# Unread identity products at four places of a hybrid decoder step: two stage ends after a feed forward and projections, one inside the index scores, one after the selection

## The chip, the cores and the metric

The kernel runs on one core of a Trainium2 chip. The metric is the device time of one execution in microseconds (us); a smaller time is better. Three executions of the kernel before took 3087.32 us in the median (3080.42 to 3089.07). A core has five engines that run side by side and wait for each other through semaphores: TensorE (PE in the profile), VectorE (DVE), ScalarE (ACT), GpSimd (POOL) and SyncE (SP), whose queue here issues most of the transfers.

## The reference

One layer of a decoder serves 1024 prompt tokens and 8 sample sequences of 4 tokens (1056 tokens in all, model width 1024).

```python
x = x + 0.5 * swiglu(rms_norm(x, ffn1_norm), ffn1_w_gate, ffn1_w_up, ffn1_w_down)      # D_FF = 2816
h = rms_norm(x, mix_norm)
q, k, v, qi, ki, wi, hq, hf, hi, hg, ga, gr = split_cols(h @ w_in)
# A: index scores I[t,s] = sum_h w[t,h] * relu(qi[t,h] . ki[s]) choose min(256, L/4) causal keys,
#    attention over the chosen keys (own keys for the prompt; paged cache plus 4 own keys for the samples)
# B: HGRN2 gated linear recurrence with a matrix state
merged = sigmoid(ga) * (att @ w_branch_attn) + sigmoid(gr) * (rec @ w_branch_hgrn)
x = x + merged @ w_out
x = x + 0.5 * swiglu(rms_norm(x, ffn2_norm), ffn2_w_gate, ffn2_w_up, ffn2_w_down)
```

Outputs are x for prompt and samples, the new keys, values, index keys, and the recurrence states.

## The kernel before

The step is a chain of stages; each stage is one `Block` with its own program for each engine, and between two Blocks stands a barrier: in the program every engine first drains what it has issued, then reports, and no engine passes before all five have reported. The profile shows the first instruction of a new Block as released by "PEq L69". The stages are: the first feed forward (tiles named `ff_`), the token projections (`tok_`), the index scores (`idx_`), the selection with further projections (`sel_`), the attention (`att_`), the recurrence (`hg_`), the merge, and the second feed forward.

Products in full precision are split: each weight and each activation is held as a high and a low part, and `split_product` (L97 to L99) issues three products for one. In the first feed forward the hidden width goes by in pairs of 128; tokens go in three chunks of 384, 384 and 288. Its last round (`LAST`) also prepares the next norm: when the down products of a chunk have been added to x (DVE, L580), ACT squares them (L341), POOL adds the squares up over eight slices (L298, `gathered`), PE sums over partitions with a product with ones (`sums`, L725), DVE makes the variance (L526) and the root, scales x (L542), and ACT and DVE write the high and low part of h (L360, L551). The last such series, for chunk 2, is the end of the stage.

The token projections go through nine weight chunks; each needs a load, ACT for the high part (L1043) and POOL for the low part (`tok_wlo`, L1001). PE starts a chunk when POOL has done it. Finished 128x256 results are turned by PE (`turn`, L1014) three steps later; the last transfer stores the turned queries.

The index scores first turn the index pages of the sample sequences on PE (`turn`, L1270) and score them (L1280), then ACT and DVE make the weighted relu of the sample part (`sample_relu`, `sample_part`, L1387, L1390), PE adds it over heads with a product with `sel` (L1308), and then come 48 steps over prompt tiles and heads: PE scores (L1322, L1324), ACT relu (L1366), DVE multiply and add (L1403, L1406).

The selection is a bisection on DVE beside 28 column blocks of projections on PE (L97 to L99, `sel_proj`). The attention begins by turning cached key pages on PE (L1772), and SP issues the loads of further pages one by one (L1679).

`idle_products` (L102 to L105) issues products of the identity with itself, 128 columns in 32-bit floats, whose result nobody reads. The kernel before has them at eight places, among them 12 at the start of the token projections, 36 and 16 in the index scores.

```python
def idle_products(nc, out, ident, count):
    for _ in range(count):
        nc.tensor.matmul(out, ident[:, :], ident[:, :], start=True, stop=True)
```

Of the kernel before, what the change touches and what calls it, by code (L numbers as in the profile page):

```python
# [29 lines left out]
P = 128  # L30
# [71 lines left out]
# [4 lines that stand above are left out]
# [3 lines left out]
QS = 2 * NCH  # L109
# [4 lines left out]
def feed_forward(nc, tag, xT, hhi, hlo, gain, w_gate, w_up, w_down, ident, ones, x_in=None, gain_row=None, next_gain=None,  # L114
# [10 lines left out]
    LAST = PAIRS - 1  # L125
    E0 = NCH if x_in is not None else 0
    with Scope(nc, tag) as s:
# [10 lines left out]
        gu = s.ps("gu", [P, 2, 2, 512])  # L138
# [544 lines left out]
        def _(pe):  # L683
# [123 lines left out]
            if next_gain is None:  # L807
                for q in range(QS):
                    gate_up(LAST, q)
            else:  # L810
                pe.wait_ge(ones_set, 1)
                for q in range(3):
                    gate_up(LAST, q)
                for j in range(KD):
                    down(LAST, j)
                gate_up(LAST, 3)
                gate_up(LAST, 4)
                sums(NCH)
                for j in range(KD, 2 * KD):
                    down(LAST, j)  # L820
                gate_up(LAST, 5)
                sums(NCH + 1)
                for j in range(2 * KD, 3 * KD):
                    down(LAST, j)
                sums(NCH + 2)
            if y_out is not None:
                n = 0
                for j in range(OUTS_PER):
                    down(LAST, j)
                    c = j // KD  # L830
                    if c and j % KD == 1 or j == OUTS_PER - 1:
                        while n < tiles_within(c - 1 if j < OUTS_PER - 1 else c):
                            turn_back(n)
                            n += 1
# [29 lines left out]
def token_projections(nc, hhi, hlo, w_in, q_gain, k_gain, cos, sin, ident, qT_d, kT_d, qiT_d, kiT_d, wi_d, hv_d,  # L864
# [10 lines left out]
    with Scope(nc, "tok") as s:  # L875
# [128 lines left out]
        @block.tensor  # L1004
        def _(pe):
            def turn(m):
                if m < 0 or m >= M or not turns(m):
                    return
                x = count(turns, m)
                if x >= 2:  # L1010
                    pe.wait_ge(kept_done, x - 1)
                pe.wait_ge(out_done, m + 1)
                for b in range(1 if kind(m) == "ki" else 2):
                    last = nc.tensor.transpose(turned[:, x % 2, b, :], out[:, m % 4, b * P:(b + 1) * P], ident[:, :])  # L1014
                last.then_inc(turn_done, 1)

            idle_products(nc, proj[:, 3, 0:P], ident, 12)
            for m in range(M):
                c, n = STEPS[m]
                w = width(c)  # L1020
                if n == 0:
                    pe.wait_ge(w_lo_done, c + 1)
                if m >= 4:
                    pe.wait_ge(take_done, m - 3)
                tok = slice(n * P, (n + 1) * P) if n < TILES else slice(T - P, T)
                for k in range(KD):
                    ps = proj[:, m % 4, 0:w]
                    nc.tensor.matmul(ps, hhi[:, k, tok], whi[:, c % WS, k, 0:w], start=(k == 0), stop=False)
                    nc.tensor.matmul(ps, hhi[:, k, tok], wlo[:, c % WS, k, 0:w], start=False, stop=False)
                    last = nc.tensor.matmul(ps, hlo[:, k, tok], whi[:, c % WS, k, 0:w], start=False, stop=(k == KD - 1))  # L1030
                last.then_inc(proj_done, 1)
                turn(m - 3)
            for m in range(M - 3, M):
                turn(m)

        @block.scalar
        def _(act):
# [140 lines left out]
def index_scores(nc, scores, qiT_d, kiT_d, wi_d, pages, pages_in, same_token, new_floor, ident):  # L1178


    with Scope(nc, "idx") as s:
# [79 lines left out]
        def _(pe):  # L1261
# [38 lines left out]
                                 lambda r: k_hi[r, cols], lambda r: k_lo[r, cols])  # L1300
                last.then_inc(seq_scored, 1)

            idle_products(nc, turned[:, 0, 0:P], ident, 16)
            pe.wait_ge(sel_in, 16)
            pe.wait_ge(sample_part, 2)
            for x in range(3):
# [105 lines left out]
FEATS = 32  # L1412


def select_keys_and_project(nc, scores, masks, hhi, hlo, w_in, feat_d, table, pages, pages_in, cache_k):

# [3 lines left out]
    with Scope(nc, "sel") as s:  # L1422
# [13 lines left out]
        bitf = s.sb("bitf", [P, SLABS])  # L1436
        thr = s.sb("thr", [P, SLABS], I32)
        proj = s.ps("proj", [P, 2, NCH, 512])
        w_loaded = [s.sem(f"w_loaded{n}") for n in range(2)]
        w_hi_done, w_lo_done = s.sem("w_hi_done"), s.sem("w_lo_done")  # L1440
        proj_done, proj_read, kept_done = s.sem("proj_done"), s.sem("proj_read"), s.sem("kept_done")
# [50 lines left out]
        @block.tensor  # L1492
        def _(pe):
            def body(n, i, pair, first):
                for u in range(2):
                    pe.wait_ge(w_lo_done, 2 * pair + u + 1)
                    for c in range(NCH):
                        cols, w_c = slice(CHUNK[c][0], CHUNK[c][0] + CHUNK[c][1]), CHUNK[c][1]
                        if not first:
                            pe.wait_ge(proj_read, 6 * pair + 3 * u + c - 5)  # L1500
                        for k in range(KD):
                            w = slice(k * P, (k + 1) * P)
                            last = split_product(nc, proj[:, u, c, 0:w_c], whi[:, u, w], wlo[:, u, w], hhi[:, k, cols],
                                                 hlo[:, k, cols], k == 0, k == KD - 1)
                        last.then_inc(proj_done, 1)

            sections(pe, body)

        @block.scalar
        def _(act):  # L1510
# [1442 lines left out]
def build(nc, a, o):  # L2953
# [9 lines left out]
    with Scope(nc, "core") as s:  # L2963
# [6 lines left out]
        with Scope(nc, "front") as front:  # L2970
# [7 lines left out]
            with Scope(nc, "proj") as proj:  # L2978
                with Scope(nc, "fetch") as fetch:
                    idx_pages = fetch.sb("idx_pages", [P, DB * PAGES, HD])  # L2980
                    token_projections(nc, hhi, hlo, a["w_in"], a["q_norm"], a["k_norm"], a["t_cos"], a["t_sin"], ident,
                                      scratch["qT"], scratch["kT"], scratch["qiT"], scratch["kiT"], scratch["wi"],
                                      scratch["hv"], rows["k_prompt"], rows["k_sample"], rows["v_prompt"], rows["v_sample"],
                                      rows["idx_k_prompt"], rows["idx_k_sample"], table, a["page_table"], idx_pages,
                                      idx_pages_in, a["cache_idx_k"])
                    scores = proj.sb("scores", [P, SLABS, SW], side="right")
                    index_scores(nc, scores, scratch["qiT"], scratch["kiT"], scratch["wi"], idx_pages, idx_pages_in,
                                 a["t_same_token"], a["t_new_floor"], ident)
                mix = Scope(nc, "mix").__enter__()
                masks = mix.sb("masks", [P, SLABS, SW], mybir.dt.bfloat16)  # L2990
                pages = mix.sb("pages", [P, SLOTS * PAGES, KV * HD])
                select_keys_and_project(nc, scores, masks, hhi, hlo, a["w_in"], scratch["feat"], table, pages, first_pages_in,
                                        cache_k)
        attention(nc, scratch["mixed"], masks, pages, first_pages_in, table, scratch["qT"], scratch["kT"], rows["v_prompt"],
                  rows["v_sample"], cache_k, cache_v, a["t_causal"], a["t_own"], ident, values_in)
        mix.__exit__(None, None, None)
# [82 lines left out]
```

## Time and profile before

| | |
|---|---|
| median of three runs | 3087.32 us (3080.42 to 3089.07) |
| the profiled execution: time, span in the trace | 3090.39 us, 3088.7 us |
| PE, DVE, ACT, POOL busy | 94%, 50%, 23%, 19% |
| mean granted TensorE clock | 0.957 |
| idle products in the trace | 956 records of 478 products |

Times in the trace are microseconds from the start of the span. A row of the order of time gives start, time taken, engine, line, operation, the tile written and the tiles read, the shape, and in brackets how long the engine had been idle and who released it. A full-precision 32-bit product is recorded as two MATMUL records. The granted clock is a share of full speed: 1.00 is 2.4 GHz, 0.50 is 1.2 GHz.

### The profile page before, as it was taken

The page shows a single profiled execution, that of the slowest core. Times are in us where ns is not written, and L with a number is a line of the kernel's source. Part 1 is how long each engine was busy: PE and PEld are TensorE (multiplying, and loading weights), DVE is VectorE, ACT ScalarE, POOL GpSimd, SP SyncE. Part 2 cuts the span into 40 slices and gives each one's busy share as a digit, 9 for nine tenths or more (in the row PEclk, how much of TensorE's full clock was granted, in tenths as well). Part 3 has the DMA queues.
Part 4 walks back from the last instruction along what each step waited for, and adds up shares of the span by engine and source line. Part 5 has one row for each costly group of instructions (what it writes and reads, how often), then busy time and mean ns, then how long its engine had stood idle before and what let it go on. Part 6 is the DMA issues. An engine that isn't in the chain of part 4 may idle for free. (4 is left out here: it accounts for less than half of the span.)

```text
span 3088.7 us, 50931 instructions
## 1 busy us (share of the span) xinstructions
PE 2907.8 (94%) x19321; PEld 2810.8 (91%) x19321; DVE 1530.8 (50%) x3429; ACT 699.6 (23%) x1351; POOL 575.5 (19%) x330
## 2 busy tenths in 40 slices
PE   8999999999699986999989988879989999999998
PEld 7999999999699965999958987778979999999998
DVE  5333322223767639999924657656444222233323
ACT  5111111111323235222113444321032111111110
POOL 0121221112311012122132111122002111122120
PEclk9999999999799998999987998789999999999999
DMA  4111111111223112243263141225211111111111
GB/s 126 42 56 53 41 54 41 41 41 41 78 78 109 47 45 55 90 144 115 86 168 94 25 144 58 75 69 159 76 49 55 41 41 41 41 48 61 41 34 57
DMA packets 239301, 212.93 MB, mean 69 GB/s; under 512 B 26978, under 2 KB 216578, under 8 KB 239042
## 3 DMA queue, kind: packets, MB, share of 16 engines
q1 hardware_dynamic: 230594, 182.35, 19.9%
q10 hardware_dynamic: 4608, 17.30, 1.4%
q0 software_dynamic: 3968, 11.54, 1.4%
q8 instruction: 81, 1.33, 0.2%
q14 instruction: 50, 0.41, 0.0%
HBM read 167.94 MB, written 43.21 MB: 68 GB/s over the span
## 5 line engine op out<-in xcount | busy, mean ns | idle before, releaser
L271 POOL TENSOR_TENSOR ff_wlo<-ff_raw,ff_whi 128x1024 fp32r<-128x1024 f32 x124 | 298.6, 2429 | 1203.6 <-ACT ff_whi L369 1202.5
L567 DVE TENSOR_TENSOR ff_prod<-ff_silu,ff_gu 128x384 f32<-128x384 f32 x132 | 68.8, 521 | 806.8 <-ACT ff_silu L374 806.8
L97 PE MATMUL ff_dn<-ff_ahi,ff_whi 128*128 128x384 f32 (+1 forms) x1056 | 340.4, 322 | 8.2 <-DVE ff_alo L573 3.8
L97 PE MATMUL ff_gu<-front_hhi,ff_whi 128*128 128x384 f32 (+1 forms) x1056 | 340.6, 323 | 2.6 <-DVE front_hlo L511 2.3
L99 PE MATMUL ff_gu<-front_hhi,ff_wlo 128*128 128x384 f32 (+1 forms) x1056 | 339.4, 321 | 0.0
L98 PE MATMUL ff_gu<-front_hlo,ff_whi 128*128 128x384 f32 (+1 forms) x1056 | 339.4, 321 | 0.0
L99 PE MATMUL ff_dn<-ff_ahi,ff_wlo 128*128 128x384 f32 (+1 forms) x1056 | 339.2, 321 | 0.0
L98 PE MATMUL ff_dn<-ff_alo,ff_whi 128*128 128x384 f32 (+1 forms) x1056 | 339.2, 321 | 0.0
L97 PE MATMUL ff_gu<-rear_hhi,ff_whi 128*128 128x384 f32 (+1 forms) x1056 | 338.8, 321 | 0.0
L98 PE MATMUL ff_gu<-rear_hlo,ff_whi 128*128 128x384 f32 (+1 forms) x1056 | 338.6, 321 | 0.0
L99 PE MATMUL ff_gu<-rear_hhi,ff_wlo 128*128 128x384 f32 (+1 forms) x1056 | 338.5, 321 | 0.0
L374 ACT ACTIVATE ff_silu<-ff_gu 128x384 f32<-128x384 f32 x132 | 61.4, 466 | 864.7 <-PE ff_gu L99 864.7
L97 PE MATMUL sel_proj<-front_hhi,sel_whi 128*128 128x384 f32 (+1 forms) x672 | 216.8, 323 | 14.5 <-POOL sel_wlo L1488 14.5
L369 ACT ACTIVATE ff_whi<-ff_raw 128x1024 fp32r<-128x1024 f32 x132 | 132.6, 1053 | 374.3 <-PE ff_dn L99 285.1
L98 PE MATMUL sel_proj<-front_hlo,sel_whi 128*128 128x384 f32 (+1 forms) x672 | 216.6, 322 | 0.0
L99 PE MATMUL sel_proj<-front_hhi,sel_wlo 128*128 128x384 f32 (+1 forms) x672 | 216.5, 322 | 0.0
L97 PEld LDWEIGHTS ff_dn<-ff_ahi,ff_whi 128*128 128x128 f32 x1056 | 198.7, 188 | 10.4 <-DVE ff_alo L573 4.4
L97 PEld LDWEIGHTS ff_gu<-front_hhi,ff_whi 128*128 128x128 f32 x1056 | 198.7, 188 | 3.1 <-DVE ff_wlo L516 3.0
L98 PEld LDWEIGHTS ff_dn<-ff_alo,ff_whi 128*128 128x128 f32 x1056 | 198.7, 188 | 0.1
L98 PEld LDWEIGHTS ff_gu<-front_hlo,ff_whi 128*128 128x128 f32 x1056 | 198.8, 188 | 0.0
L99 PEld LDWEIGHTS ff_dn<-ff_ahi,ff_wlo 128*128 128x128 f32 x1056 | 198.7, 188 | 0.0
L99 PEld LDWEIGHTS ff_gu<-front_hhi,ff_wlo 128*128 128x128 f32 x1056 | 198.7, 188 | 0.0
(336 smaller groups left out, 6236.9 us busy)
## 6 DMA issues: line engine op xcount, KB each, us to landing
ff_raw<-in_ffn_w_gate SPq DMA_DIRECT2D x44, 512.0 KB, 3.7
ff_raw<-in_ffn_w_up SPq DMA_DIRECT2D x44, 512.0 KB, 3.7
ff_raw<-in_ffn_w_down SPq DMA_DIRECT2D x44, 512.0 KB, 3.4
scratch_feat<-sel_stage ACTq DMA_DIRECT2D x32, 528.0 KB, 2.7
sel_raw<-in_w_in SPq DMA_DIRECT2D x28, 512.0 KB, 3.7
merge_gates<-scratch_feat SPq DMA_DIRECT2D x48, 176.0 KB, 2.7
tok_raw<-in_w_in SPq DMA_DIRECT2D x8, 1024.0 KB, 6.5
mix_pages<-in_cache_k SPq DMA_DIRECT2D x64, 128.0 KB, 2.1
```

Of the source, the lines that this page charges most:

```text
L97: nc.tensor.matmul(out, w_hi, x_hi, start=first, stop=False)
L98: nc.tensor.matmul(out, w_hi, x_lo, start=False, stop=False)
L99: return nc.tensor.matmul(out, w_lo, x_hi, start=False, stop=last)
L271: nc.gpsimd.tensor_tensor(wlo[:, u, :], raw[:, u % RAW, :], whi[:, u, :], ALU.subtract).then_inc(w_lo_done, 1)
L369: nc.scalar.activation(whi[:, u, :], raw[:, u % RAW, :], ACT.Copy).then_inc(w_hi_done, 1)
L374: nc.scalar.activation(act_out[:, q % 2, 0:w], gu[:, q % 2, 0, 0:w], ACT.Silu).then_inc(silu_done, 1)
L567: nc.vector.tensor_tensor(prod[:, 0:w], act_out[:, b, 0:w], gu[:, b, 1, 0:w], ALU.mult).then_inc(prod_done, 1)
```

## The change

`idle_products` is called at five more points, and one call grows. In the first feed forward's last round 26 are put before the last eight down products (behind a wait that `prod_done` has reached the fifth product of that round), 28 after them, and 84 after the last `sums`. At the end of the token projections stand 30, behind a wait for `take_done`. In the index scores the 16 before the product with `sel` become 76. At the end of the selection stand 26, into a bank of PSUM that is added for them.

```diff
@@ feed_forward, block.tensor
                 gate_up(LAST, 5)
                 sums(NCH + 1)
+                pe.wait_ge(prod_done, QS * LAST + 5)
+                idle_products(nc, gu[:, 0, 0, 0:P], ident, 26)
                 for j in range(2 * KD, 3 * KD):
                     down(LAST, j)
+                idle_products(nc, gu[:, 0, 0, 0:P], ident, 28)
                 sums(NCH + 2)
+                idle_products(nc, gu[:, 0, 0, 0:P], ident, 84)
@@ token_projections, block.tensor
             for m in range(M - 3, M):
                 turn(m)
+            pe.wait_ge(take_done, M - 3)
+            idle_products(nc, proj[:, M % 4, 0:P], ident, 30)
@@ index_scores, block.tensor
-            idle_products(nc, turned[:, 0, 0:P], ident, 16)
+            idle_products(nc, turned[:, 0, 0:P], ident, 76)
             pe.wait_ge(sel_in, 16)
             pe.wait_ge(sample_part, 2)
@@ select_keys_and_project
         proj = s.ps("proj", [P, 2, NCH, 512])
+        unread = s.ps("unread", [P, 512])
...
             sections(pe, body)
+            idle_products(nc, unread[:, 0:P], ident, 26)
```

`ident` is handed to `select_keys_and_project` as one more argument. No other engine's program changes, and no transfer.

The order of PE's instructions at the end of the first feed forward (`ff_`) and the start of the token projections (`tok_`), before; the two branches are the passage from Block to Block with its barrier:

```order
1346 L99 MATMUL ff_dn<-ff_ahi,ff_wlo 128x288
1347 L725 MATMUL ff_dn<-ff_raw,core_ones 128x288
1348 L69 UNCONDITIONAL_BRANCH
1349 L1004 UNCONDITIONAL_BRANCH
1350 L105 MATMUL tok_proj<-core_ident 128x128 x12
```

The same place now:

```order
1347 L99 MATMUL ff_dn<-ff_ahi,ff_wlo 128x288
1348 L105 MATMUL ff_gu<-core_ident 128x128 x28
1349 L725 MATMUL ff_dn<-ff_raw,core_ones 128x288
1350 L105 MATMUL ff_gu<-core_ident 128x128 x84
1351 L69 UNCONDITIONAL_BRANCH
1352 L1008 UNCONDITIONAL_BRANCH
1353 L105 MATMUL tok_proj<-core_ident 128x128 x12
```

28 products have moved in before the last sums, and 84 between the sums and the barrier.

PE in the index scores (`idx_`), between the last sample sequence and the product with `sel`, before:

```order
3428 L1280 MATMUL idx_big<-idx_k_hi,idx_wide_lo 128x4 x2
3429 L105 MATMUL idx_turned<-core_ident 128x128 x16
3430 L1308 MATMUL idx_big<-idx_relus,idx_sel 128x512 x2
3431 L1308 MATMUL idx_big<-idx_relus,idx_sel 128x4
3432 L1322 MATMUL idx_big<-idx_k_hi,idx_q_both 128x384
```

and now:

```order
3432 L1286 MATMUL idx_big<-idx_k_hi,idx_wide_lo 128x4 x2
3433 L105 MATMUL idx_turned<-core_ident 128x128 x76
3434 L1314 MATMUL idx_big<-idx_relus,idx_sel 128x512 x2
3435 L1314 MATMUL idx_big<-idx_relus,idx_sel 128x4
3436 L1328 MATMUL idx_big<-idx_k_hi,idx_q_both 128x384
```

The order is the same; 60 more products stand ahead of the product with `sel`.

## Rows read from the trace of the kernel before

**Rows 1.** The page: PE's busy time, and its granted clock in 40 slices.

```profile
PE 2907.8 (94%) x19321; PEld 2810.8 (91%) x19321; DVE 1530.8 (50%) x3429; ACT 699.6 (23%) x1351; POOL 575.5 (19%) x330
PEclk9999999999799998999987998789999999999999
```

**Rows 2.** Instructions in order of time, PE, end of the first feed forward.

```profile
790.50 0.81 PE L725 MATMUL ff_dn<-ff_raw,core_ones 128*128 128x384 f32 x2
795.09 0.40 PE L97 MATMUL ff_dn<-ff_ahi,ff_whi 128*128 128x288 f32 x1 [3.78 <-DVE ff_alo L573]
...
805.42 0.30 PE L98 MATMUL ff_dn<-ff_alo,ff_whi 128*128 128x288 f32 x1
805.56 0.29 PE L99 MATMUL ff_dn<-ff_ahi,ff_wlo 128*128 128x288 f32 x1
810.78 1.33 PE L725 MATMUL ff_dn<-ff_raw,core_ones 128*128 128x288 f32 x2 [4.93 <-POOL ff_raw L298]
822.55 4.86 PE L105 MATMUL tok_proj<-core_ident 128*128 128x128 f32 x24 [10.44 <-PEq L69]
...
839.99 0.58 PE L1028 MATMUL tok_proj<-tok_whi,front_hhi 128*128 128x256 f32 x1 [2.28 <-POOL tok_wlo L1001]
```

**Rows 3.** The same view, DVE, same stretch.

```profile
798.75 0.82 DVE L580 SCALAR_TENSOR_TENSOR x_xT<-ff_dn,x_xT 128x288 f32<-128x288 f32 x2
...
812.27 0.44 DVE L526 TENSOR_SCALAR ff_room<-ff_dn 128x288 f32<-128x288 f32 x1
...
819.55 2.67 DVE L551 TENSOR_TENSOR front_hlo<-ff_room,front_hhi 128x1152 fp32r<-128x1152 f32 x2
```

**Rows 4.** PE across the passage from token projections to index scores.

```profile
1089.76 0.41 PE L1014 MATMUL tok_turned<-core_ident,tok_out 128*128 128x128 f32 x2 [0.73 <-DVE tok_out L1152]
1095.02 3.68 PE L1270 MATMUL idx_turned<-core_ident,fetch_idx_pages 128*64 128x128 f32 x32 [4.86 <-PEq L69]
1098.63 8.81 PE L105 MATMUL idx_big<-core_ident 128*128 128x128 f32 x72
1107.37 1.97 PE L1270 MATMUL idx_turned<-core_ident,fetch_idx_pages 128*64 128x128 f32 x32
```

**Rows 5.** PE in the index scores, before and after the product with `sel`.

```profile
1135.12 3.84 PE L105 MATMUL idx_turned<-core_ident 128*128 128x128 f32 x32
1146.34 3.97 PE L1308 MATMUL idx_big<-idx_relus,idx_sel 128*128 128x512 f32 x6 [7.38 <-DVE idx_relus L1390]
1150.56 0.59 PE L1322 MATMUL idx_big<-idx_k_hi,idx_q_both 128*128 128x384 f32 x1 [0.25 <-DVE proj_scores L1394]
```

**Rows 6.** PE, end of the selection and start of the attention.

```profile
1540.68 0.29 PE L99 MATMUL sel_proj<-front_hhi,sel_wlo 128*128 128x288 f32 x1
1545.46 1.94 PE L1772 MATMUL att_turned<-core_ident,mix_pages 128*128 128x128 f32 x8 [4.48 <-PEq L69]
```

**Rows 7.** PE in the recurrence: idle products at full clock and what follows them.

```profile
2043.41 1.95 PE L105 MATMUL hg_kd_ps<-core_ident 128*128 128x128 f32 x16
2045.20 0.27 PE L2643 MATMUL hg_kd_ps<-core_ident,hg_kd 128*128 128x128 f32 x1
```

**Rows 8.** DVE, start of the index scores.

```profile
1103.95 1.27 DVE L1383 TENSOR_TENSOR idx_past_lo<-idx_turned,idx_past_hi 128x512 fp32r<-128x512 f32 x2
```

**Rows 9.** Windows: length; PE, PEld, DVE, ACT, POOL busy (instructions); clock, DMA, GB/s.

```profile
830.00:840.00 10.00, 7.72 (x38) 7.58 (x37) 4.43 (x1) 4.06 (x4) 4.58 (x2) 0.50 0.56 184
1146.00:1150.00 4.00, 3.66 (x6) 1.63 (x6) 0.19 (x1) 0.00 (x0) 0.00 (x0) 0.50 0.46 124
1160.00:1200.00 40.00, 30.67 (x126) 20.87 (x127) 36.51 (x35) 28.78 (x37) 9.79 (x9) 1.00 0.16 40
1545.00:1553.00 8.00, 6.47 (x27) 5.40 (x28) 3.15 (x5) 1.78 (x3) 0.00 (x0) 0.50 0.75 155
```

**Rows 10.** Order of time, DVE at the selection's end, then SP in the attention.

```profile
1544.50 0.43 DVE L1598 TENSOR_SCALAR mix_masks<-sel_over 128x1028 bf16<-128x1028 bf16 x1
1560.09 35.22 SPq L1679 DMA_DIRECT2D mix_pages<-in_cache_k  x32
```

More of the change, by code:

```diff
@@ L1412, with select_keys_and_project @@
 FEATS = 32
-def select_keys_and_project(nc, scores, masks, hhi, hlo, w_in, feat_d, table, pages, pages_in, cache_k):
+def select_keys_and_project(nc, scores, masks, hhi, hlo, w_in, feat_d, table, pages, pages_in, cache_k, ident):
     with Scope(nc, "sel") as s:
@@ L2992, in build @@
                 select_keys_and_project(nc, scores, masks, hhi, hlo, a["w_in"], scratch["feat"], table, pages, first_pages_in,
-                                        cache_k)
+                                        cache_k, ident)
         attention(nc, scratch["mixed"], masks, pages, first_pages_in, table, scratch["qT"], scratch["kT"], rows["v_prompt"],
```

## The prediction

> **What bounds the kernel now.** I read the page first: PE is busy for 94% of the span, and its clock row has dips at the passages between stages [rows 1]. So what PE does is mostly the time, and at the passages I asked for the order of time of every engine, engine by engine, since there PE waits for the others. The reader is to see two things at each of the four places: when PE becomes free and when the next thing is due that needs it.
>
> End of the first feed forward: PE idles 3.78 us before 795.09, 4.93 us before 810.78, and 10.44 us before 822.55, where the next Block starts [rows 2]. DVE is the engine that holds that stretch: it is adding and scaling without a break from 795 on and ends at 819.55 + 2.67 = 822.22 [rows 3]; PE starts the new Block 0.33 us later. End of the token projections: PE's last turn begins at 1089.76, the Block changes at 1095.02 after the last store has landed [rows 4]. Index scores: PE is idle for 7.38 us ahead of the product with `sel`, waiting for DVE [rows 5]. End of the selection: PE issues its last product at 1540.68, DVE ends at 1544.50 + 0.43 = 1544.93, and the attention starts at 1545.46 [rows 6, 10].
>
> The change fills these holes. All depends on what one product costs against the length of each hole.
>
> **The price of one product.** 12 calls of the program appear as 24 records [rows 2], 36 as 72 [rows 4], 16 as 32 [rows 5]: two records each. At full clock 16 records (8 products) take from 2043.41 to 2045.20, 1.79 us [rows 7], so 0.224 us a product. The 16 products at 1135.12 bear it out: 3.84 us, 0.24 us each with the tail of the last [rows 5]. At 1.2 GHz 12 products took 4.86 us, 0.4 us each [rows 2]. The stretches filled here begin at full clock with PE just out of dense work, so I use 0.224 us.
>
> **Feed forward, 26 products before the last down products.** The wait ahead of them is for a product of DVE that was over long before. They begin at about 791.0 and take 26 x 0.224 = 5.8 us, to 796.9. The down products then start 1.8 us later than at 795.09, but at full clock (six products a result, 0.14 us from start to start as at 805.42 and 805.56 [rows 2], so 0.8 us for each of the eight results): the first two are done at about 797.8 and 798.6. DVE takes them at 798.75 [rows 3], since it has other work until then. So: 0, at most 0.3 us.
>
> **28 products before the last sums.** PE's last down product begins at 805.56; 28 x 0.224 = 6.3 us lead to 812.0. The sums began at 810.78 and took 1.33 us at half clock [rows 2], to 812.1; now 812.0 + 0.67 = 812.7. DVE's next step on them stood at 812.27 [rows 3]. About 0.4 us later on DVE, and hidden by the next item.
>
> **84 products before the barrier.** They begin at 812.5 and take 84 x 0.224 = 18.8 us, to 831.3. Every engine passes the barrier only when PE has drained. DVE is done at 822.6, so the hole holds about 45 products; the rest stick out. With the 0.33 us of the passage the token projections start at 831.6 instead of 822.55: **+9.1 us**. What comes back? The first loads of that Block are issued behind the barrier, so they move with it. Before, PE ran its first small products at half clock, 7.72 us busy in the 10 us from 830 to 840 [rows 9], yet it then still waited 2.28 us for POOL's `tok_wlo` until 839.99 [rows 2]. A fast clock there only lengthens that wait. Only products after 839.99 could gain, up to 0.8 us; after a new wait the clock will be low there again. I take 0; ends 8.3 and 9.7.
>
> **30 products at the end of the token projections.** 1090.0 + 6.7 = 1096.7; the passage then is at about 1097.1 instead of 1095.02, 2.1 us late. Here the clock pays: PE went through its first 32 records in 1098.63 - 1095.02 = 3.6 us and does the same 32 in 1.97 us once the clock is up, and the old 36 products took 8.74 us instead of 8.1 [rows 4]. Now 1097.1 + 1.9 + 8.1 = 1107.1, where it was 1107.37. DVE's part needed next was ready at 1103.95 + 1.27 = 1105.2 [rows 8] and moves to 1107.3. Sum **+0.1 us**; ends -0.5 (DVE part faster) and 2.1 (nothing returned).
>
> **76 instead of 16 in the index scores.** 1135.12 + 76 x 0.224 (17.0) = 1152.1. The product with `sel` could start at 1146.34 and is queued behind them: 5.8 us late. It took 3.97 us at half clock [rows 5, 9]; at full clock it takes half, 2.0 us back. The first prompt scores behind it (0.59 us for one at half clock) give 0.2 more. DVE and ACT wait for exactly this product, and from then on DVE is 36.5 us of 40 busy [rows 9], so the delay passes on: **+3.6 us**; ends 2.9 and 5.8.
>
> **26 at the end of the selection.** 1540.8 + 5.8 = 1546.6, and 0.2 for the last one; DVE was done at 1544.93. The attention starts at about 1547.2 instead of 1545.46: **+1.7 us**. PE was at half clock there for 8 us with 6.47 us busy [rows 9], so up to 3.2 us could come back. But SP issues the 32 page loads one after the other for 35.22 us from 1560.09 [rows 10], all behind the barrier, and PE's later turns wait for these pages; SP's start moves with the barrier whatever PE's clock is. I take 1.7; ends -1.5 and 2.2.
>
> **Sum.** 9.1 + 0.1 + 3.6 + 1.7 = 14.5 us. The profiled execution took 3090.39 us, 3.1 us above the median of its runs, so it would take 3104.9; against the median 3087.3 + 14.5 = 3101.8, which I give as 3102.
>
> **Rivals.**
> *The clock pays on the path.* Here the lifted clock shortens the stage by half of all PE work now done cold at the four places: 7.72 + 3.66 + 6.47 in the windows of [rows 9], 3.68 in [rows 4], 4.86 and 1.33 in [rows 2], 27.7 us, so 13.9 back. The delays before any return are 9.1 + 2.1 + 5.8 + 1.7 = 18.7; +4.8, a time of 3092, not slower by what can be told. For it: the index part really pays back its half. Against it: in the two largest pieces PE waits afterwards for POOL and SP [rows 2, 10]. It decides if those waits shrink, too. The Trainium skill, page "TensorE: Matmul & The Clock Gate", section "Terms", gives this rule: the penalty of a throttled stretch is about its length times the missing share of the clock. By that rule the change would come out near this time; the rows speak against it wherever another engine ends the wait.
>
> *The barrier does not wait for the unread products.* If the others pass while PE still runs its queue, the end of the feed forward costs nothing: PE is through at 831.3, does the 12 old products until 834.0, and its small products, which took at most 837.7 - 827.4 = 10.3 us mostly at half clock [rows 2], in under 6 us, so before 840. Token end -0.5, selection 0, index scores still 3.6: +3.1, 3090. Against it: the program has a drain on PE ahead of its report.
>
> *One product costs one record, 0.112 us.* Then 84 take 9.4 us, 76 take 8.5, 30 take 3.4, and every hole holds its filling; the product with `sel` gives 2.2 back, the start of the index scores up to 2.1: -4.3, 3083. Against it stand three counts of records [rows 2, 4, 5].
>
> **How the numbers follow.** My forecast 0.82; the clock on the path 0.06; no wait at the barrier 0.06; the half price 0.03; 0.03 for more than the sum, as when the clock is low during the 84 or the later stages meet their transfers worse. The forecast's own range is 3096 to 3107: the ends of the parts, not all at once, and about 3 us of spread between runs. To leave out less than 2 in 10 I widen it slightly, to 3095 to 3108. A measurement of this kernel tells about 0.3% (9.3 us) from no change, so slower means above 3096.6: nearly all of the forecast, 0.82 in all. Within: 0.14. Faster by over 0.3% (below 3078): 0.04.
>
> **What would show it.** In the profile after: 168 records of 128x128 ahead of the first Block passage, with about 0.11 us between starts and the clock at 1.00; DVE idle for 9 us with the passage as its releaser; the first product of the second weight chunk 9 us later; the product with `sel` 15.0 us later at its start (9.1 + 0.1 + 5.8) and 13 us later at its end, in 2.0 us; DVE idle longer ahead of the index scores' prompt part; SP's page loads about 14.5 us later. It would be wrong if SP or DVE start the token projections while these products still run, if a product takes under 0.15 us, or if the attention starts late but the second feed forward does not.

## The result, and the profile after

The changed kernel takes 3102.68 us (median of 6 runs, 3095.11 to 3106.0), the kernel before on the same chip 3087.6 us (6 runs, 3080.42 to 3091.54). The ratio is 1.0048, with a 95% interval of 1.0038 to 1.0058: 11.7 to 17.9 us slower. The forecast was 3102.

The page of the changed kernel, the two lines that answer to [rows 1]:

```profile
PE 2952.4 (95%) x19829; PEld 2858.4 (92%) x19829; DVE 1530.1 (49%) x3429; ACT 699.4 (23%) x1351; POOL 575.1 (19%) x330
PEclk9999999999999998999997998879999999999999
```

PE has 508 more instructions, two for each of the 254 added calls (26 + 28 + 84 + 30 + 60 + 26). PE is busier by 44.6 us and its clock row has fewer dips, and the kernel is slower. Work that nobody reads counts as busy; the share of PE says nothing about this change.

The end of the feed forward, instructions of PE in order of time, after (start, duration, engine, line, operation; in brackets the idle time before and what ended it). They answer to [rows 2]:

```profile
797.21 0.38 PE L97 MATMUL ff_dn<-ff_ahi,ff_whi 128*128 128x288 f32 x1
...
806.03 6.41 PE L105 MATMUL ff_gu<-core_ident 128*128 128x128 f32 x56
812.28 0.65 PE L725 MATMUL ff_dn<-ff_raw,core_ones 128*128 128x288 f32 x2
812.76 18.92 PE L105 MATMUL ff_gu<-core_ident 128*128 128x128 f32 x168
831.99 2.92 PE L105 MATMUL tok_proj<-core_ident 128*128 128x128 f32 x24 [0.30 <-PEq L69]
838.03 0.43 PE L1032 MATMUL tok_proj<-tok_whi,front_hhi 128*128 128x72 f32 x1 [3.13 <-POOL tok_wlo L1005]
...
849.40 0.58 PE L1032 MATMUL tok_proj<-tok_whi,front_hhi 128*128 128x256 f32 x1 [0.92 <-POOL tok_wlo L1005]
```

PE waits for `tok_wlo` twice here, ahead of the first weight chunk (products of 72 columns) and ahead of the second (256 columns). [rows 2] has only the second of before, 2.28 us; the first is this row of PE in before:

```profile
828.58 0.30 PE L1028 MATMUL tok_proj<-tok_whi,front_hhi 128*128 128x72 f32 x1 [1.16 <-POOL tok_wlo L1001]
```

So the first wait grew from 1.16 to 3.13 us, and the second shrank from 2.28 to 0.92, since the 72-column products between the two waits took longer: behind the longer first wait they ran at a granted clock of 0.50 from the first on, in before at 1.00 up to 829.9 and at 0.50 after that. Counted from the passage, the first chunk starts at 6.03 us in before and 6.04 in after, the second at 17.44 and 17.41.

DVE in the same stretch, answering to [rows 3] (after), and its first instruction of the new Block in before:

```profile
799.09 0.82 DVE L580 SCALAR_TENSOR_TENSOR x_xT<-ff_dn,x_xT 128x288 f32<-128x288 f32 x2
...
812.97 0.46 DVE L526 TENSOR_SCALAR ff_room<-ff_dn 128x288 f32<-128x288 f32 x1 [0.27 <-PE ff_dn L725]
...
820.26 2.68 DVE L551 TENSOR_TENSOR front_hlo<-ff_room,front_hhi 128x1152 fp32r<-128x1152 f32 x2
...
844.97 4.46 DVE L1105 TENSOR_TENSOR tok_ra<-tok_taken,tok_cs 128x64 f32<-128x64 f32 x1 [22.04 <-ACT tok_taken L1076]
```

```profile
835.57 4.45 DVE L1099 TENSOR_TENSOR tok_ra<-tok_taken,tok_cs 128x64 f32<-128x64 f32 x1 [13.34 <-ACT tok_taken L1070]
```

All of this execution stands 0.34 us later than in before (790.84 against 790.50 at the sums of the second chunk). DVE is done at 822.94, PE at 831.68, and the passage follows PE 0.30 us later. The other engines wait for products that no engine reads.

The passage to the index scores, PE, then DVE, answering to [rows 4, 8]:

```profile
1099.89 6.86 PE L105 MATMUL tok_proj<-core_ident 128*128 128x128 f32 x60
1107.05 1.97 PE L1276 MATMUL idx_turned<-core_ident,fetch_idx_pages 128*64 128x128 f32 x32 [0.30 <-PEq L69]
...
1118.36 1.97 PE L1276 MATMUL idx_turned<-core_ident,fetch_idx_pages 128*64 128x128 f32 x32 [1.11 <-DVE idx_past_lo L1389]
```

```profile
1110.99 0.23 DVE L1380 COPY idx_relus<-idx_q_new 128x128 f32<-128x128 f32 x1 [2.75 <-DMA idx_q_new<-scratch_qiT]
```

The first 32 records of pages are fast (1.97 us instead of 3.68), but the second turn now waits 1.11 us for DVE's `idx_past_lo`. DVE had waited 2.75 us for a load, but that load is not what held the turn: behind its copy DVE waits another 3.18 us for ACT. The first instruction of ACT in the stage waits for another load, the index keys (`scratch_kiT`). ACT in before and in after:

```profile
1099.32 1.08 ACT L1338 ACTIVATE idx_k_hi<-idx_relus 128x1056 fp32r<-128x1056 f32 x1 [8.90 <-DMA idx_relus<-scratch_kiT]
```

```profile
1112.31 1.08 ACT L1344 ACTIVATE idx_k_hi<-idx_relus 128x1056 fp32r<-128x1056 f32 x1 [11.99 <-DMA idx_relus<-scratch_kiT]
```

That is 4.30 us behind the passage in before and 5.26 us in after. ACT then writes the high part of the queries, DVE its low part (`idx_wide_lo`) and `idx_past_lo`, and PE's second turn follows 6.05 us behind that first instruction of ACT.

The product with `sel`, PE and then DVE, answering to [rows 5], and last DVE in before:

```profile
1146.11 17.24 PE L105 MATMUL idx_turned<-core_ident 128*128 128x128 f32 x152
1163.19 2.00 PE L1314 MATMUL idx_big<-idx_relus,idx_sel 128*128 128x512 f32 x6
```

```profile
1165.23 0.16 DVE L1400 TENSOR_TENSOR proj_scores<-idx_big,idx_floor 128x4 f32<-128x4 f32 x1 [8.17 <-PE idx_big L1314]
```

```profile
1150.35 0.16 DVE L1394 TENSOR_TENSOR proj_scores<-idx_big,idx_floor 128x4 f32<-128x4 f32 x1 [4.16 <-PE idx_big L1308]
```

DVE waits 8.17 us for it; before, 4.16 us. The product has no idle time ahead of it: it is queued behind PE's own filling.

The end of the selection, PE, then DVE and SP, answering to [rows 6, 10]:

```profile
1555.38 5.97 PE L105 MATMUL sel_unread<-core_ident 128*128 128x128 f32 x52
1561.64 1.07 PE L1780 MATMUL att_turned<-core_ident,mix_pages 128*128 128x128 f32 x8 [0.30 <-PEq L69]
```

```profile
1561.89 0.94 DVE L1966 MEMSET att_wide<- 128x1056 f32 x1 [2.38 <-PEq L69]
...
1576.21 35.18 SPq L1687 DMA_DIRECT2D mix_pages<-in_cache_k  x32
```

DVE waits 2.38 us at this passage; where PE is not late it waits 0.78 us.

By stages, counted from the sums of the second chunk (790.50 in before), each cut at the first instruction behind the passage (of PE, and of DVE for the selection) or at the second turn of the pages. The second pair is the same two programs, profiled once more:

| part | forecast | after less before | second pair |
| --- | --- | --- | --- |
| sums to token projections | +9.1 | +9.10 | +9.11 |
| token projections to the second turn of pages | +0.1 | +1.55 | +0.76 |
| to the start of the selection | +3.6 | +3.88 | +4.03 |
| selection to attention | +1.7 | +1.31 | +0.85 |
| attention to the end of the span | 0 | -5.5 | -0.5 |
| sum | 14.5 | 10.4 | 14.2 |

The first term is wrong by no more than 0.01 us. What comes behind the attention scatters from one execution to the next: in the 14 profiles taken it lasts 1534.4 to 1545.1 us, without order by what was changed. So I compare medians for the whole, and traces only up to the attention.

Does the clock pay in the attention, which the forecast put at nothing? PE, the first wait for a page load, in before and in after:

```profile
1588.19 1.09 PE L1772 MATMUL att_turned<-core_ident,mix_pages 128*128 128x128 f32 x8 [0.93 <-DMA mix_pages<-in_cache_k]
```

```profile
1604.29 1.09 PE L1780 MATMUL att_turned<-core_ident,mix_pages 128*128 128x128 f32 x8 [1.49 <-DMA mix_pages<-in_cache_k]
```

That is 42.73 and 42.65 us behind the start of the attention (42.53 and 43.09 in the second pair): up to there nothing is returned. The whole attention, up to PE's first product of the recurrence, lasted 255.4 us in both profiles of before and 251.1 and 252.8 in those of the changed kernel. Below, the selection's products alone left it at 255.2, and two kernels without any of them (the doubled and the moved filling) had 252.1 and 252.6. So these 3 to 4 us don't follow the products at the selection's end; what makes them is open.

### The profile page after: what moved, and what is told of

Same layout as the page of the kernel before. It is cut to its first block and busy times, and to the rows that moved or that the text cites. A ratio compares the mean times of both kernels' runs of the same rounds, so it can differ in the third digit from the quotient of the medians.

```text
span 3099.4 us, 51947 instructions
## 1 busy us (share of the span) xinstructions
PE 2952.4 (95%) x19829; PEld 2858.4 (92%) x19829; DVE 1530.1 (49%) x3429; ACT 699.4 (23%) x1351; POOL 575.1 (19%) x330
## 5 line engine op out<-in xcount | busy, mean ns | idle before, releaser
L97 PE MATMUL sel_proj<-front_hhi,sel_whi 128*128 128x384 f32 (+1 forms) x672 | 216.9, 323 | 14.5 <-POOL sel_wlo L1495 14.5
L97 PEld LDWEIGHTS ff_gu<-rear_hhi,ff_whi 128*128 128x128 f32 x1056 | 198.3, 188 | 0.1
```

Source lines behind the costliest of these rows:

```text
L97: nc.tensor.matmul(out, w_hi, x_hi, start=first, stop=False)
```

## The experiments

Each diff is against the kernel before unless it says otherwise; in all, the selection has the tile for the unread products. A median is over 5 to 12 runs of the variant (4 for the one with double products, one for each second profile), beside 15 or 29 runs of the kernel before (one for the second profiles).

**The feed forward alone.**

```
+                pe.wait_ge(prod_done, QS * LAST + 5)
+                idle_products(nc, gu[:, 0, 0, 0:P], ident, 26)
...
+                idle_products(nc, gu[:, 0, 0, 0:P], ident, 28)
                 sums(NCH + 2)
+                idle_products(nc, gu[:, 0, 0, 0:P], ident, 84)
```

> The kernel before with only the 26, 28 and 84 unread products of the first feed forward. Theory (the barrier waits until PE has drained, a product costs 0.224 us): the token projections start 9.1 us later than in the kernel before, measured from the same product in the last round, everything behind is shifted by this, whole time +9.1 us. Rival (the barrier does not wait for unread products): token projections start at the old place, time +0. Rival (a fast clock shortens the path by half of the work that was cold): start +9.1, but about 6.5 us returned by the first full chunk of the token projections, time +2 to +3.

Measured: 3095.52 us against 3086.84, ratio 1.0028 [1.0017, 1.0039], 5.2 to 12.0 us slower. The trace has +9.09 us from the sums to the token projections, and then again PE waiting for POOL ahead of the first chunk, 3.45 us instead of 1.16:

```profile
812.39 18.92 PE L105 MATMUL ff_gu<-core_ident 128*128 128x128 f32 x168
831.61 2.92 PE L105 MATMUL tok_proj<-core_ident 128*128 128x128 f32 x24 [0.30 <-PEq L69]
837.98 0.43 PE L1032 MATMUL tok_proj<-tok_whi,front_hhi 128*128 128x72 f32 x1 [3.45 <-POOL tok_wlo L1005]
```

More than half of the slowdown is here, and nothing of it is returned: the second chunk starts 17.56 us behind the passage, in before 17.44. Both rivals (+0, and +2 to +3 with 6.5 us back by then) fall.

**The index scores alone.**

```
-            idle_products(nc, turned[:, 0, 0:P], ident, 16)
+            idle_products(nc, turned[:, 0, 0:P], ident, 76)
```

> The kernel before with only the unread products inside the index scores raised from 16 to 76. Theory: the product with sel starts 5.8 us later, takes 2.0 instead of 4.0 us, and DVE passes the rest on: the selection starts 3.6 to 3.9 us later, time +3.6. Rival (DVE and ACT have slack in the prompt part and catch up): start of sel +5.8, start of the selection +1 or less, time +0 to 1.

Measured: 3091.07 against 3086.84, ratio 1.0012 [1.0003, 1.0021]. In the trace the second turn of pages is at 1106.70 and the product with `sel` starts at 1151.52 and takes 2.00 us; from the turn to the selection it is 3.9 us longer than in before. The delay of a queued product minus what the clock returns, as forecast.

**The selection alone.**

```
+            idle_products(nc, unread[:, 0:P], ident, 26)
```

> The kernel before with only the 26 unread products at the end of the selection. Theory: the attention starts 1.7 us later and SP's page loads with it, and PE's earlier full clock saves nothing behind the page loads: time +1.7. Rival (the clock pays in the attention): start +1.7, but the sample part of the attention is 1.5 to 3 us shorter, time -1.5 to 0.

Measured: 3084.07 against 3086.84, ratio 0.9994 [0.9985, 1.0003], 4.6 us faster to 0.9 slower: the expected +1.7 did not come. PE in the trace:

```profile
1539.21 5.97 PE L105 MATMUL sel_unread<-core_ident 128*128 128x128 f32 x52
1545.94 1.06 PE L1774 MATMUL att_turned<-core_ident,mix_pages 128*128 128x128 f32 x8 [0.75 <-PEq L69]
```

The 26 products end at 1545.18, DVE at 1545.41: here the hole held them, and the attention starts as in before. The rival's gain in the attention isn't in this trace either (255.2 us up to the recurrence, 255.4 in before); the times leave it open. In the first profile of the changed kernel the hole did not hold them (PE idle for 0.30 us, so PE was last). The hole has two lengths, see the last section.

**The token projections alone.**

```
+            pe.wait_ge(take_done, M - 3)
+            idle_products(nc, proj[:, M % 4, 0:P], ident, 30)
```

> The kernel before with only the 30 unread products at the end of the token projections. Theory as predicted: the passage to the index scores is 2.1 us late, the fast clock behind it gives it all back, the second turn of index pages starts 0.1 us late, time +0.1. Rival, from the profile of the changed kernel: the first transfers of the index scores (idx_q_new, idx_relus) land later by 1 to 2 us once the passage has moved, so the second turn starts 1.1 us late, time +1.1.

Measured: 3088.29 against 3086.67, ratio 1.0008 [0.9999, 1.0016]. PE:

```profile
1096.08 1.97 PE L1272 MATMUL idx_turned<-core_ident,fetch_idx_pages 128*64 128x128 f32 x32 [0.30 <-PEq L69]
...
1106.55 1.97 PE L1272 MATMUL idx_turned<-core_ident,fetch_idx_pages 128*64 128x128 f32 x32 [0.27 <-DVE idx_past_lo L1385]
```

DVE waits 0.82 us for `idx_q_new`, as in before. From the sums on (this execution stands 0.92 us early), the passage is 1.98 us late and the second turn 0.10 us: in this profile the part is what I forecast. The rival's +1.1 is inside the interval of the times (0.3 us faster to 4.9 slower), and the other profiles with the 30 products have more, see below.

**Twice the products before the barrier** (168 instead of 84, feed forward alone).

> First feed forward with 26, 28 and 168 products, twice the 84; the rest as before. Theory: each product beyond about 45 moves the barrier by 0.224 us, so the token projections start 9.1 + 84 x 0.224 = 27.9 us late, time +28. Rival (the clock is lowered in a long run of unread products, or part of them is dropped): 84 more at the price of half clock, 0.4 us each, +43; or less than +20.

Measured: 3116.28 against 3086.67, ratio 1.0096 [1.0077, 1.0115]. PE, and the stretch as a window (length, PE, PEld, DVE, ACT, POOL busy with their instructions, clock, DMA share, GB/s):

```profile
812.32 37.68 PE L105 MATMUL ff_gu<-core_ident 128*128 128x128 f32 x336
850.30 2.92 PE L105 MATMUL tok_proj<-core_ident 128*128 128x128 f32 x24 [0.30 <-PEq L69]
```

```profile
813.00:850.00 37.00, 37.00 (x332) 36.81 (x330) 9.35 (x15) 3.22 (x4) 0.00 (x0) 1.00 0.01 2
```

The stage is 27.87 us longer than before, against 9.09 with 84: 84 more products cost 18.78 us, 0.2236 us each. By the medians it is 23.8 to 35.5 us slower (+28 expected). Both rivals named for this run fall (+43 or less than +20), and two of the prediction's: a barrier that does not wait would give nothing, half the price half of it.

**39 of the 84 moved behind the barrier** (feed forward alone, 45 there, and 51 instead of 12 where the token projections start).

```
-            idle_products(nc, proj[:, 3, 0:P], ident, 12)
+            idle_products(nc, proj[:, 3, 0:P], ident, 51)
```

> Where do surplus products cost? First feed forward with 26, 28 and 45 products (45 fill the hole), and the 39 that are left of the 84 put behind the barrier, at the start of the token projections (51 instead of 12). The index scores, the ends of the token projections and of the selection as before. Theory (they cost because the other engines stand at the barrier): the passage is at most 0.5 us late, the 51 products end before 835, the small products behind them before 840.5, when the weights of the next chunk are ready anyway: time 0 to +0.5, or -0.8 where the clock is still full at 840. Rival (39 products cost their 8.7 us wherever they stand): time +9.

Measured: 3085.44 against 3086.67, ratio 0.9998 [0.9989, 1.0007], 3.4 us faster to 2.2 slower: the 9 us are gone, with the same number of products on PE. From the sums to the token projections it is 0.39 us longer than before. The cost is not the work but the side of the barrier on which it stands: behind it PE alone is late, and there it has to wait for POOL's weights anyway. In this trace PE goes into the second chunk without a wait, 18.8 us behind the passage (17.4 in before); its weights came 1.3 us later, too (ACT began their high part 12.2 us behind the passage instead of 10.9). The token projections are 2.5 us longer than in before, in the 14 profiles they vary by over 4 us, so the trace alone does not show that nothing is lost; the medians do, to 2.2 us.

**Each place filled to its hole** (14, 18 and 38 in the feed forward; 14 at the end of the token projections; 44 in the index scores; 14 at the end of the selection).

> The changed kernel with the counts cut to what each hole holds at 0.224 us a product: 14, 18, 38 in the feed forward (26, 28, 84), 14 at the end of the token projections (30), 44 in the index scores (76), 14 at the end of the selection (26). Theory: no passage is late; the start of the index scores returns 2.1 us and the product with sel 2.2 us: time -4.3 us against the kernel before, -19 against the changed one. Rival (unread products themselves disturb other engines or the later stages): still slower than the kernel before, +3 or more.

Measured: 3082.01 against 3086.84, ratio 0.9984 [0.9975, 0.9993], faster than before by 2.2 to 7.7 us. PE at two of the places, to be held against [rows 2, 4, 5]:

```profile
823.85 4.38 PE L105 MATMUL tok_proj<-core_ident 128*128 128x128 f32 x24 [2.54 <-PEq L69]
...
1094.84 1.97 PE L1276 MATMUL idx_turned<-core_ident,fetch_idx_pages 128*64 128x128 f32 x32 [1.74 <-PEq L69]
...
1144.03 2.07 PE L1314 MATMUL idx_big<-idx_relus,idx_sel 128*128 128x512 f32 x6 [0.98 <-DVE idx_relus L1396]
```

At both passages PE still waits (2.54 and 1.74 us), so nobody waits for it; the first turn and the product with `sel` are as fast as in the changed kernel, and now at their own time. The feed forward's part is 0.00 us longer than before; from the token projections to the selection it is 5.4 us shorter (380.79 against 386.19). Here the clock does pay, 1.7 us at the first turn and 1.9 at the product with `sel`; the token projections, without an edit inside, were 1.5 us shorter in this execution, which is within their scatter (3.9 us without them; the interval of the medians holds both).

**The same idea with more behind the barrier** (14, 18, 42; 51 instead of 12 at the start of the token projections; 18; 48; 14).

> The sized kernel of before (14, 18, 38; 14; 44; 14) with the holes filled further: 14, 18, 42 in the feed forward, 51 instead of 12 at the start of the token projections, 18 at their end, 48 in the index scores, 14 at the end of the selection. Theory: passages not late by more than 0.3 us; like the sized kernel -4.5 us against the kernel before, and 0.8 us more if the clock stays full until the first full chunk of the token projections. Rival (a hole is overfilled somewhere): slower than the sized kernel by 0.5 us or more.

Measured: 3080.94 against 3086.67, ratio 0.9982 [0.9973, 0.9991]. It beats before by 2.8 to 8.3 us, and is not to be told from the version with 14, 18 and 38. PE at the passage to the index scores:

```profile
1087.61 4.18 PE L105 MATMUL tok_proj<-core_ident 128*128 128x128 f32 x36
1093.94 3.63 PE L1276 MATMUL idx_turned<-core_ident,fetch_idx_pages 128*64 128x128 f32 x32 [2.15 <-PEq L69]
```

18 products there kept nothing warm: PE was idle for 2.15 us and the first turn took 3.63 us at a granted clock of 0.53, where after 14 products and 1.74 us of idle time it took 1.97 at 1.00.

**Both kernels profiled a second time**, without an edit.

> The kernel before, unchanged, profiled once more, to see how far the stages differ between two executions of one program. By my theory the stages up to the attention repeat within 3 us (product with the selection matrix at 1146.3, attention at 1545.5) and the later ones scatter by 2 to 4 us, since where PE's clock dips there is not set by the change. If the later stages repeat within 1 us instead, the differences that I saw behind the attention belong to the change.

> The changed kernel, unchanged, profiled once more. My theory: the token projections start 9.1 us later than the feed forward's first sums would have it (41.2 us behind them), the product with the selection matrix takes 2.0 us, the attention starts 14 to 16 us later than in before. The idle time of DVE ahead of idx_q_new, 2.75 us in the first profile, was chance: here it should be about 1.8 us (its passage 1 us late or less against what the clock gives), and the second turn of the pages come 1 us earlier than in the first profile. The rival: the late landing belongs to the change, and 2.75 us come again. The span is then between 3098 and 3106 us by either.

Measured: 3085.25 and 3100.28 us, 15.0 apart. The last column of the table above is from them. The stages up to the attention repeat (the first within 0.01 us, each other one within 0.6 us in before and 1.4 in the changed kernel), the later part does not (1543.2 and 1539.7 us for one program). DVE waits 2.01 us for `idx_q_new` in the changed kernel and 0.84 us in before. That is near the 1.8 us that I expected for chance, but more than any of the ten profiles of other kernels showed up to then (0.79 to 0.98).

**Feed forward and token projections together**, to settle that.

> The products of the feed forward (26, 28, 84) and the 30 at the end of the token projections together, the index scores and the selection as in before. In both profiles of the changed kernel DVE waited 2.0 and 2.75 us for idx_q_new, in the ten others 0.79 to 0.98 us, also with either of these two parts alone. Theory: the parts add up, the wait is 0.8 to 1.0 us here, the second turn of pages comes 9.2 us after its place in before for the same start of the first sums, and the time is 9.1 + 0.1 = 9.2 us above before. Rival: the two together make that load late; the wait is 2.0 us or more, the second turn comes 10 us or more later, and the time is 10 to 11 us above before.

Measured: 3096.46 against 3085.56, ratio 1.0036 [1.0022, 1.0049]. DVE:

```profile
1112.14 0.23 DVE L1380 COPY idx_relus<-idx_q_new 128x128 f32<-128x128 f32 x1 [2.31 <-DMA idx_q_new<-scratch_qiT]
```

The wait is 2.31 us, as the rival has it. All three profiles that have the 84 and the 30 together have the long wait (2.01, 2.31, 2.75 us), the eleven others, also with either alone, 0.79 to 0.98 us. Why this load lands later is open. But it isn't what makes the second turn late. The turn comes 11.8 us late, of which 9.1 are the barrier, 2.0 longer token projections (269.2 us up to PE's last turn, 267.2 in before, 265.3 to 269.7 in all profiles), and 0.7 what lies between the last turn and the second turn of the pages. What holds the second turn is ACT's wait for the index keys: in the six profiles where the first turn is fast, it follows the first instruction of ACT by 6.05 or 6.06 us, whatever DVE's wait for `idx_q_new` was. The next run shows it best.

**The change without the feed forward** (30, 76 and 26).

> The changed kernel without the products of the first feed forward: 30, 76 and 26 at the three later places. Theory: 0.1 + 3.6 + 1.7 = 5.4 us above before, the attention starts 5.4 us later than in before for the same start of the token projections. Rival: 26 products at the end of the selection cost nothing here either, as when they stood alone and ended before DVE; then the attention starts 3.7 us later and the time is 3.7 us above before. With the 9.1 us of the feed forward this should give the 14.5 to 15 us of the whole change.

Measured: 3088.76 against 3085.56, ratio 1.0009 [1.0000, 1.0018]. ACT at the start of the index scores:

```profile
1101.35 1.08 ACT L1340 ACTIVATE idx_k_hi<-idx_relus 128x1056 fp32r<-128x1056 f32 x1 [12.64 <-DMA idx_relus<-scratch_kiT]
```

DVE's wait for `idx_q_new` is short here (0.92 us), yet ACT starts 5.90 us behind the passage and the second turn waits 1.76 us for DVE, the longest of all. So the late second turn needs neither the 84 products nor the late `idx_q_new`. Without the 30 products ACT started 4.25 to 4.75 us behind the passage (nine profiles), with them 4.41 to 5.90 (five). Why the keys land later in some of these is open.

PE at the end of the selection:

```profile
1544.87 5.97 PE L105 MATMUL sel_unread<-core_ident 128*128 128x128 f32 x52
1551.14 1.06 PE L1776 MATMUL att_turned<-core_ident,mix_pages 128*128 128x128 f32 x8 [0.30 <-PEq L69]
```

Here PE ends last again, at 1550.84 with DVE done at 1548.98, and the attention starts 5.5 us later than in before for the same start of the sums (forecast 5.4, rival 3.7). By the trace the selection's part came as the theory has it; that the whole came so near is in part luck, since 1.8 us more between the last turn and the second turn stand against token projections 1.9 us shorter. By the times both hold (0 to 5.6 us). In the traces, up to the attention, this and the feed forward alone (+10.2) add up to 15.7 us, the whole change has 15.8 and 14.8. The ratios add up to 11.4 us (8.6 and 2.8), the whole change has 14.8 (11.7 to 17.9); the difference is within the uncertainty of the three ratios.

## Why the prediction came out right, step by step

- **The price, 0.224 us a product**: right. 84 more cost 18.78 us, and 168 records last 18.92 us.
- **26 and 28 products**: right. The down products begin at 797.21 (796.9 and the 0.34 of this execution), DVE takes them where it did, and its step on the last sums is 0.36 us later for the 0.4 of the forecast.
- **84 before the barrier, +9.1**: right to 0.01 us, also alone (9.09) and doubled (27.87). That nothing comes back is shown too: the unread products at the start are faster (24 records in 2.92 us instead of 4.86), and the wait for `tok_wlo` behind them is 3.13 us instead of 1.16. The prediction had the wait the wrong way round in one point: it said that a fast clock would lengthen the wait ahead of the second chunk (2.28 us), but that wait shrank to 0.92, because the products between ran at half clock. Both chunks start where POOL's weights come, so the term stays at 0. The rule of the Trainium skill, page "TensorE: Matmul & The Clock Gate", section "Terms", that a throttled stretch costs its length times the missing share, would by an estimate give back half of these 4.86 us, 2.4 us; the trace does not agree with it where another engine ends the wait. At the product with `sel` it does: 3.97 us at half clock, 2.00 at full.
- **30 products, +0.1**: the mechanism was right, the size off. Counted from PE's last turn the passage is 2.1 us late (2.3 to 2.6 from the start of the stage) and the 32 records take 1.97 us, but the second turn is 0.8 to 1.6 us late (0.6 to 1.1 without the scatter of the token projections). The step that put DVE's part at 1107.3 moved it along with the passage from one trace. Its chain hangs on the load of the index keys, and ACT could start 4.4 to 5.9 us behind the passage in the five profiles with these products, where it was 4.30 in before. From PE's last turn to the second turn of the pages these five took 17.9 to 19.4 us (18.5 in the mean), seven profiles without products there 17.1 to 18.1 (17.6): about 0.8 us instead of 0.1. The 0.10 of this part alone is the best of the five.
- **76 products, +3.6**: 3.9 and 4.0 measured. The start of the product with `sel` moved by 5.86 us from the second turn on (5.8), and it took 2.00 us. The announced sums of 15.0 us at its start and 13 at its end were 16.9 and 14.9, larger by the 0.34 us of this execution and by the 1.5 us of the step before.
- **26 products at the selection's end, +1.7**: right for one of two courses. Where DVE ended 4.1 us behind PE's last product, the passage was 1.6 us late (2.38 - 0.78 and 2.41 - 0.78), where it ended 6.2 us behind, not at all. The step that took DVE's end from one trace took a number that has two values. SP's page loads did move, by 16.1 us, with the attention's start, and PE waits for them at the same distance behind it; so nothing came back up to there.
- **One sign was put wrong**: DVE's idle time at the first passage is not ended by the passage but by ACT's `tok_taken`; it is 22.04 us instead of 13.34, longer by 8.7. The delay goes through the passage, but the row names only the last thing waited for.

The first and the third term, 12.7 of the 14.5 us, are right for the reason given. That the sum is so near is partly luck: the second term was 0.7 to 1.5 us too small and the fourth 0.4 to 0.9 too large in these two pairs, and whole executions differ by several us (the first pair 10.4 apart, the second 14.2). One small slip in the chances: the rivals' times, 3092, 3090 and 3083, all lie within 0.3% of no change, so nothing named stood behind the 0.04 for faster.

## What to carry to other kernels

Filling that keeps TensorE's clock up must end before the thing that it waits for, and by some margin: every product that sticks out ahead of a barrier delays all engines at its full price, and one that stands ahead of a queued product on the path delays that. Count the hole from when PE becomes free to when the last other engine is done, divide by the price of a product at full clock, and take fewer; what does not fit can stand behind the barrier, as far as PE has to wait for weights there. Read a hole from more than one profile: one of those filled here was 4.5 us long in some and 6.6 in others. A faster clock pays only where the next thing on the path is PE's own.

## What the runs showed of the hardware that I had not expected

**The clock can fall while PE has no gap.** In the kernel with 51 products behind the barrier PE goes over to products of 72 columns at 835.56, and from 838.74 on each of them starts 0.21 us behind the last instead of 0.11. PE in order of time, and windows (columns as above):

```profile
838.46 0.28 PE L1034 MATMUL tok_proj<-tok_whi,front_hlo 128*128 128x72 f32 x1
838.57 0.36 PE L1032 MATMUL tok_proj<-tok_whi,front_hhi 128*128 128x72 f32 x1
838.74 0.41 PE L1033 MATMUL tok_proj<-tok_wlo,front_hhi 128*128 128x72 f32 x1
```

```profile
831.00:836.00 5.00, 5.00 (x47) 5.00 (x47) 0.00 (x0) 0.00 (x0) 0.00 (x0) 1.00 1.03 348
838.00:840.00 2.00, 2.00 (x14) 2.00 (x14) 1.23 (x1) 1.45 (x3) 1.66 (x1) 0.66 0.02 7
840.00:842.00 2.00, 2.00 (x11) 2.00 (x11) 2.00 (x1) 0.95 (x1) 2.00 (x1) 0.50 0.00 0
```

PE is busy for the whole of each window by the records, and the granted clock goes from 1.00 to 0.50. In the kernel with doubled filling 332 records of 128 columns ran for 37 us at 1.00.

**DVE's selection has two courses.** In the loops of the selection some of DVE's smallest operations (128x7) take 1.9 to 2.4 us where the others of their kind take about 0.17, 12 of them in the 340 us, at the same distance from the end in some profiles and at other ones in the rest. DVE in before, and in the kernel with the 30 products alone:

```profile
1496.41 0.17 DVE L1581 TENSOR_TENSOR sel_gain<-sel_gain,sel_bitf 128x7 int32<-128x7 int32 x1
1496.61 2.35 DVE L1582 TENSOR_TENSOR sel_bits<-sel_bits,sel_gain 128x7 int32<-128x7 int32 x1
```

```profile
1473.62 2.38 DVE L1580 TENSOR_TENSOR sel_cand<-sel_bits,sel_bit 128x7 int32<-128x7 int32 x1 [0.39 <-DVE sel_bitf L1587]
```

With the last such operation 48.8 us before the attention (before, both times) PE's hole at the passage is 4.47 to 4.50 us; with it 73.9 us before (30 alone) it is 6.57 us, as in two more profiles, and nothing between was seen. The changed kernel showed DVE's end 4.1 us behind PE's last product in its first profile and 6.2 in its second, so the change doesn't choose the course. What makes these operations long was not tried.
